# Shifting the activation pages of a transformer kernel by 32 bytes a partition

## The chip, the cores and the metric

The kernel runs on one core of one Trainium2 chip. The metric is the device time of one execution in microseconds. Before the change the median of 3 runs is 3561.03 us (3560.19 to 3562.94).

## What is computed

The reference is three transformer layers over 512 tokens of width 1024, in float32. Each of the first two layers (`hybrid_layer`) is a SwiGLU feed-forward, a mixer of three branches (a gated delta rule, a sliding-window attention, a cross attention over 256 memory rows), and a second SwiGLU, each with a layer norm. The third layer has a mixer of four attention branches and a convolutional feed-forward:

```python
def swiglu(x, w_gu, w_down):
    gate, up = jnp.split(x @ w_gu, 2, axis=-1)
    return (jax.nn.silu(gate) * up) @ w_down
...
h = layer_norm(DEEPNORM_ALPHA * x + 0.5 * swiglu(x, ffn1_w_gu, ffn1_w_down), ln_g[0], ln_b[0])
... = jnp.split(h @ w_in, split_idx, axis=-1)
merged = jnp.sum(gates * jnp.einsum('bsnc,ncd->bsnd', branches, w_branch), axis=2)
h = layer_norm(DEEPNORM_ALPHA * h + merged @ w_out, ln_g[1], ln_b[1])
return layer_norm(DEEPNORM_ALPHA * h + 0.5 * swiglu(h, ffn2_w_gu, ffn2_w_down), ln_g[2], ln_b[2])
```

Nearly all arithmetic is dense products of a weight matrix with an activation of 1024 or 2816 rows by 512 tokens.

## The kernel before

**Products.** Activations are kept transposed: a tile is 128 features (partitions) by 512 tokens, 2048 bytes a partition. A weight block is 128 by 128. Every float32 operand of a dense product is split into a rounded part (hi) and a rest (lo), both in the type float32r, and a block product is three matmuls: hi by hi, hi by lo, lo by hi. `block_matmuls` (lines 2490, 2491, 2499) issues them with 512 columns:

```python
self.e.matmul(o, hi, X.hi[kt], start=first, stop=False)
self.e.matmul(o, hi, X.lo[kt], start=False, stop=False)
...
last = self.e.matmul(o, lo, X.hi[kt], start=False, stop=final)
```

The second argument is the stationary operand (weights, from `w_hi` or `w_lo`), the third the moving operand, 128 partitions by 512 columns of a page. `pair_matmuls` (lines 2525, 2527, 2528) does the same with 256 columns, for products that are made of half tiles and sums of weight blocks; `half_matmuls` (lines 2509 to 2511) does it for the last output tile. Some blocks have two further matmuls with four columns of the tile `gains` (lines 2497, 2498). Small matmuls of attention and norms are plain float32 (lines 2473, 2478, 2536, 2568, 2596, 2609 and others).

**Memory.** `Memory.__init__` allocates the memory of each partition from low to high addresses, in the order of the code; a tensor's size is rounded up to 32 bytes. `w_lo` and `raw` (the same 14 units of 2048 bytes) begin at byte 16512, `w_hi` (9 units) at 45184, the constants `cst` at 63616. These three are multiples of 128. After `par` (1784 bytes, so 1792), `alb` (192), `small` (8192), `tab` (32), `mean_rounded` (512) and `gains` (768) come the pages: 71 tiles of 2048 bytes, each with two names, `page_f` (float32) and `page_r` (float32r). The first begins at byte 83808, which is 654 times 128 plus 96; the others follow at steps of 2048 bytes, so every page begins 96 bytes past a multiple of 128. The last ends at 229216. Nothing is allocated behind the pages.

**Who uses pages.** The moving operand of every split product is a page. ScalarE and VectorE read and write pages in norms, activations and attention. DMA touches them seldom: SyncE's queue loads the eight input tiles, the memory rows and the bias tiles and writes most of the output, ScalarE's queue moves a few half tiles. The weights go to `raw` units by 864 loads on SyncE's queue, and as pairs on SyncE's and GpSimd's.

**Order.** The work around the products is set by a planner (`Pace`) with fixed costs in the code (`BLOCK_US`, `GAIN_US`); it does not see addresses. Pages are handed out by `Stock` in the order of their numbers and of their release. A weight slab of four blocks is loaded to a `raw` unit, rounded to `w_hi` by ScalarE (line 2813), its rest written over `raw` by VectorE (line 3235), and then multiplied.

Of the kernel before, what the change touches and what calls it, by code (L numbers as in the profile page):

```python
# [13 lines left out]
P = 128  # L14
# [27 lines left out]
BESIDE = 6  # L42
HALF = (slice(0, 256), slice(256, 512))
PAGES = 71
CONST_PARTS = 4
NGAIN = 48
UNIT = SLAB * P
# [64 lines left out]
class Lane:  # L112
# [3 lines left out]
    def __init__(self, sems):  # L116
        self.tensor, self.scalar, self.vector = sems
        self.raised = [0, 0, 0]
# [311 lines left out]
class Memory:  # L430


    def __init__(self, nc, ctx, w, pairs, x_t, mem_t, consts, params, table, buckets, out):
        def sb(name, shape, dt=F32):
            return ctx.enter_context(nc.sbuf_tensor(name, shape, dt))

        def sem(name):
            return ctx.enter_context(nc.semaphore(name))

        self.pairs = pairs  # L440
        self.nc, self.w, self.x_t, self.mem_t, self.consts, self.params = nc, w, x_t, mem_t, consts, params
        self.table, self.buckets, self.out = table, buckets, out
        with nc.sbuf_tensor("w_lo", [P, NRAW * UNIT], F32R) as lo:
            self.w_lo = lo
        self.raw = sb("raw", [P, NRAW * UNIT])
        with nc.sbuf_tensor("w_lent", [P, NHI * UNIT], F32) as lent:
            self.w_lent = lent
        self.w_hi = sb("w_hi", [P, NHI * UNIT], F32R)
        self.cst = sb("cst", [P, NCONST])
        self.par = sb("par", [P, NPARAM])  # L450
        self.alb = sb("alb", [P, 48])
        self.small = sb("small", [P, 2048])
        self.tab = sb("tab", [33, 8])
        self.mean_rounded = sb("mean_rounded", [P, P], F32R)
        self.gains = sb("gains", [P, 4 * NGAIN], F32R)
        self.page_aps = []
        for i in range(PAGES):
            with nc.sbuf_tensor(f"page_r{i}", [P, 512], F32R) as r:
                rounded = r
            self.page_aps.append((sb(f"page_f{i}", [P, 512]), rounded))  # L460
        self.bank_aps = [ctx.enter_context(nc.psum_tensor(f"bank{i}", [P, 512], F32)) for i in range(8)]
        self.scratch = nc.dram_tensor("bias_rows", (8, P, 640), F32, kind="Internal").ap()

        self.lane_sems = {k: tuple(sem(f"{k}_{e}") for e in ("tensor", "scalar", "vector")) for k in LANES}
        self.s_raw = [sem(f"slab_landed{i}") for i in range(NRAW)]
        self.s_added = [sem(f"slab_added{i}") for i in range(NRAW)]
        self.s_hi, self.s_lo, self.s_gemm = sem("slab_rounded"), sem("slab_rest"), sem("blocks_multiplied")
        self.s_cst, self.s_par, self.s_tab = sem("consts_landed"), sem("params_landed"), sem("table_landed")
        self.s_x = [sem(f"x_landed{i}") for i in range(8)]
        self.s_mem = [sem(f"mem_landed{i}") for i in range(8)]  # L470
        self.s_onehot, self.s_keys, self.s_out = sem("onehot_landed"), sem("keys_landed"), sem("out_written")
        self.s_rows = [sem(f"bias_rows_written{i}") for i in range(8)]
        self.s_tile = [sem(f"bias_tile_landed{i}") for i in range(8)]
# [10 lines left out]
class Order:  # L484
# [739 lines left out]
    def prepare_memory(self):  # L1224
        for i in range(CONST_PARTS):
            self.load_constants(i)
# [1241 lines left out]
class Tensor(Engine):  # L2468
# [12 lines left out]
    def constants_ready(self):  # L2481
        self.wait_ge(self.m.s_cst, 16 * CONST_PARTS)

# [297 lines left out]
class Scalar(Engine):  # L2781
# [16 lines left out]
    def constants_ready(self):  # L2798
        self.wait_ge(self.m.s_cst, 16 * CONST_PARTS)
        self.wait_ge(self.m.s_par, 16)  # L2800
# [406 lines left out]
class Vector(Engine):  # L3207
# [6 lines left out]
    def constants_ready(self):  # L3214
        a, n = PARAM_AT["ln_b"]
        self.wait_ge(self.m.s_cst, 16 * CONST_PARTS)
        self.wait_ge(self.m.s_par, 16)
# [585 lines left out]
class Sync(Engine):  # L3803
# [11 lines left out]
    def load_constants(self, i):  # L3815
        a, b = i * NCONST // CONST_PARTS, (i + 1) * NCONST // CONST_PARTS
        self.e.dma_start(self.m.cst[:, a:b], self.m.consts[:, a:b]).then_inc(self.m.s_cst, 16)
        if i == 0:
            self.e.dma_start(self.m.par[:, :], self.m.params).then_inc(self.m.s_par, 16)
            self.wait_ge(*self.setup["table"])  # L3820
            self.e.dma_start(self.m.tab[0:32, :], self.m.table).then_inc(self.m.s_tab, 16)
# [155 lines left out]
```

## Time and profile before

| | us |
|---|---|
| median of 3 runs | 3561.03 |
| lowest, highest | 3560.19, 3562.94 |
| span of the profiled execution | 3557.1 |
| TensorE busy | 3502.0 |
| VectorE busy | 2226.9 |
| ScalarE busy | 1679.6 |

The profile is of one execution. Its page gives the span from first to last instruction and no separate time for that execution; the median lies 3.9 us above the span, which is what lies around it. The ends of matmuls are modelled, so a matmul's duration in the profile is not its share of the engine; the distance from one start to the next is.

### The profile page before, as it was taken

The numbers are of one execution on the slowest core, as the hardware profiler recorded it, in microseconds if no ns is written. First come the engines' busy times: TensorE is split into PE (matmuls) and PEld (weight loads), VectorE is DVE, ScalarE is ACT, GpSimd is POOL, SyncE is SP. The second block draws the span as 40 slices with busy tenths as digits, with TensorE's granted clock in tenths as the row PEclk, the third lists the DMA queues.
The fourth block names the chain that finished last, engine by engine and source line by source line (L and its number), as shares of the span: only waits on it lengthen the run. The fifth ranks groups of instructions, "written<-read, shape, count | busy, mean of one in ns | idle before, by whom it ended". The sixth has DMA issues, their size and how long they took to land.

```text
span 3557.1 us, 49763 instructions
## 1 busy us (share of the span) xinstructions
PE 3502.0 (98%) x19256; PEld 2932.2 (82%) x19256; DVE 2226.9 (63%) x4229; ACT 1679.6 (47%) x3243; POOL 111.3 (3%) x132
## 2 busy tenths in 40 slices
PE   9999999999999999999999999999999999999999
PEld 7898878877888987998888877888977677788887
DVE  5566656556775667566665566765676786666643
ACT  5354455554353545454555543553455443444432
POOL 0010000000000100010000000001000000000000
PEclk9999999999999999999999999999999999999999
DMA  5474331112335743574221112255522222233332
GB/s 154 131 175 143 116 95 48 45 47 72 90 105 138 173 122 98 140 172 125 83 66 47 47 60 91 93 134 151 152 79 86 69 66 84 77 94 93 95 95 86
DMA packets 198276, 358.86 MB, mean 101 GB/s; under 512 B 22102, under 2 KB 26359, under 8 KB 198040
## 3 DMA queue, kind: packets, MB, share of 16 engines
q1 hardware_dynamic: 178840, 321.32, 29.8%
q0 software_dynamic: 18432, 33.56, 5.6%
q8 instruction: 153, 2.51, 0.3%
q10 hardware_dynamic: 768, 0.79, 0.1%
q14 instruction: 83, 0.68, 0.1%
HBM read 350.60 MB, written 4.72 MB: 100 GB/s over the span
## 4 chain that ended last, share of the span: by engine, by line
PE 93%; DVE 4%; ACT 2%; issue 1%; DMA 0%; DVEq 0%; ACTq 0%
PE bank L2490 21%; PE bank L2499 21%; PE bank L2491 21%; PE bank L2525 6%; PE bank L2527 6%; PE bank L2528 6%; PE bank L2478 2%; PE bank L2473 1%; PE bank L2568 1%; PE bank L2661 1%; PE bank L2671 1%; PE bank L2536 1%; PE bank L2759 1%; PE bank L2588 1%; DVE w_lo L3235 0%
## 5 line engine op out<-in xcount | busy, mean ns | idle before, releaser
L2490 PE MATMUL bank<-page_r,w_hi 128*128 128x512 f32 (+1 forms) x3446 | 1383.4, 401 | 21.9 <-DVE w_lo L3235 14.7
L2499 PE MATMUL bank<-page_r,w_lo 128*128 128x512 f32 (+1 forms) x3446 | 1359.7, 395 | 0.0
L2491 PE MATMUL bank<-page_r,w_hi 128*128 128x512 f32 (+1 forms) x3446 | 1349.8, 392 | 0.0
L2490 PEld LDWEIGHTS bank<-page_r,w_hi 128*128 128x128 f32 x3446 | 650.0, 189 | 182.5 <-DVE w_lo L3235 18.8
L2813 ACT ACTIVATE w_hi<-raw 128x512 fp32r<-128x512 f32 x864 | 532.8, 626 | 558.3 <-PE bank L2499 550.1
L2499 PEld LDWEIGHTS bank<-page_r,w_lo 128*128 128x128 f32 x3446 | 649.2, 188 | 145.7
L2491 PEld LDWEIGHTS bank<-page_r,w_hi 128*128 128x128 f32 x3446 | 649.9, 189 | 141.6 <-issue 3.6
L3235 DVE TENSOR_TENSOR w_lo<-raw,w_hi 128x512 fp32r<-128x512 f32 x864 | 574.9, 686 | 150.2 <-ACT w_hi L2813 149.8
L2525 PE MATMUL bank<-page_r,w_hi 128*128 128x256 f32 x1792 | 503.7, 281 | 2.5 <-DVE w_lo L3253 2.5
L2528 PE MATMUL bank<-page_r,w_lo 128*128 128x256 f32 x1792 | 503.4, 281 | 0.0
L2527 PE MATMUL bank<-page_r,w_hi 128*128 128x256 f32 x1792 | 503.4, 281 | 0.0
L2525 PEld LDWEIGHTS bank<-page_r,w_hi 128*128 128x128 f32 x1792 | 337.7, 188 | 3.9 <-ACT page_f L2842 3.2
L2527 PEld LDWEIGHTS bank<-page_r,w_hi 128*128 128x128 f32 x1792 | 337.6, 188 | 0.7
L2528 PEld LDWEIGHTS bank<-page_r,w_lo 128*128 128x128 f32 x1792 | 337.7, 188 | 0.0
L3325 DVE SCALAR_TENSOR_TENSOR page_f<-bank,page_f 128x512 f32<-128x512 f32 x96 | 66.3, 691 | 261.6 <-PE bank L2499 260.6
L3253 DVE TENSOR_TENSOR w_lo<-raw,w_hi 128x1024 fp32r<-128x1024 f32 x192 | 228.8, 1220 | 0.0
L2822 ACT ACTIVATE w_hi<-raw 128x1024 fp32r<-128x1024 f32 x192 | 202.2, 1056 | 43.0 <-DVE raw L3247 21.3
L3799 POOL DMA_DIRECT2D raw<-pairs x128 | 111.1, 892 | 2425.4 <-DMA raw<-pairs 2424.0
L2842 ACT ACTIVATE page_f<-bank 128x256 f32<-128x256 f32 x128 | 49.2, 384 | 208.5 <-PE bank L2528 208.5
L2885 ACT ACTIVATE page_f<-page_f 128x512 f32<-128x512 f32 (+1 forms) x81 | 48.4, 604 | 130.8 <-DVE page_f L3325 112.6
L3776 DVE SCALAR_TENSOR_TENSOR page_f<-bank,par,page_f 128x511 f32<-128x511 f32 x88 | 65.5, 749 | 60.7 <-ACT page_f L3195 59.1
L2982 ACT ACTIVATE page_f<-bank 128x256 f32<-128x256 f32 (+3 forms) x129 | 45.4, 392 | 104.8 <-PE bank L2478 104.5
(322 smaller groups left out, 3462.9 us busy)
## 6 DMA issues: line engine op xcount, KB each, us to landing
raw<-weights SPq DMA_DIRECT2D x864, 256.0 KB, 2.7
raw<-pairs SPq DMA_DIRECT2D x320, 256.0 KB, 3.3
raw<-pairs POOLq DMA_DIRECT2D x128, 256.0 KB, 5.8
page_f<-x_t SPq DMA_DIRECT2D x8, 256.0 KB, 5.2
bias_rows<-page_f SPq DMA_DIRECT2D x8, 256.0 KB, 2.0
page_f<-bias_rows SPq DMA_DIRECT2D x8, 256.0 KB, 3.9
out_t<-page_f SPq DMA_DIRECT2D x12, 128.0 KB, 1.8
cst<-consts SPq DMA_DIRECT2D x4, 272.0 KB, 3.5
```

The lines of the kernel that those rows point to most:

```text
L2478: last = self.e.transpose(b.tile(i), ap[:, i * P:(i + 1) * P], self.const("ident"))
L2490: self.e.matmul(o, hi, X.hi[kt], start=first, stop=False)
L2491: self.e.matmul(o, hi, X.lo[kt], start=False, stop=False)
L2499: last = self.e.matmul(o, lo, X.hi[kt], start=False, stop=final)
L2525: self.e.matmul(b.cols(256), hi.r[:, c], x_hi, start=first and kt == 0, stop=False, skip_group_check=not first)
L2527: self.e.matmul(b.cols(256), hi.r[:, c], x_lo, start=False, stop=False, skip_group_check=not first)
L2528: last = self.e.matmul(b.cols(256), lo.r[:, c], x_hi, start=False, stop=kt == 3, skip_group_check=not first)
L2813: self.e.activation(hi.r, raw.f, ACT.Copy).then_inc(self.m.s_hi, 1)
L2822: self.e.activation(dst[0].wide_rounded(), src[0].wide(), ACT.Copy).then_inc(p.prep.lane.scalar, 1)
L3235: self.e.tensor_tensor(raw.r, raw.f, hi.r.bitcast(F32), ALU.subtract).then_inc(self.m.s_lo, 1)
L3253: self.e.tensor_tensor(src[0].wide_rounded(), src[0].wide(), hi[0].wide_rounded().bitcast(F32), ALU.subtract).then_inc(p.prep.lane.vector, 1)
L3799: self.e.dma_start(unit.f, self.m.pairs[p.number, QUARTERS.index(part)], accum_op=ALU.add) \
```

## The change

A tile `line_end` of 8 float32 values a partition (32 bytes) is allocated between `gains` and the pages. No instruction reads or writes it. The first page begins at byte 83840, which is 655 times 128 (327 times 256, plus 128), and each following page 2048 bytes later; the last ends at 229248. No instruction is added, removed or moved.

```diff
@@ -42,6 +42,7 @@
 PAGES = 71
+LINE_END = 8
 CONST_PARTS = 4
@@ -453,6 +454,7 @@
         self.mean_rounded = sb("mean_rounded", [P, P], F32R)
         self.gains = sb("gains", [P, 4 * NGAIN], F32R)
+        self.line_end = sb("line_end", [P, LINE_END])
         self.page_aps = []
```

## Rows read from the trace of the kernel before

**Rows 1.** The page, parts 1 and 2: busy time of the engines, granted clock in 40 slices.
```profile
PE 3502.0 (98%) x19256; PEld 2932.2 (82%) x19256; DVE 2226.9 (63%) x4229; ACT 1679.6 (47%) x3243; POOL 111.3 (3%) x132
...
PEclk9999999999999999999999999999999999999999
```

**Rows 2.** The page, part 4: chain of work that ended last, by engine and line.
```profile
PE 93%; DVE 4%; ACT 2%; issue 1%; DMA 0%; DVEq 0%; ACTq 0%
PE bank L2490 21%; PE bank L2499 21%; PE bank L2491 21%; PE bank L2525 6%; PE bank L2527 6%; PE bank L2528 6%; PE bank L2478 2%; PE bank L2473 1%; PE bank L2568 1%; PE bank L2661 1%; PE bank L2671 1%; PE bank L2536 1%; PE bank L2759 1%; PE bank L2588 1%; DVE w_lo L3235 0%
```

**Rows 3.** Groups by line and shape: the split matmuls, xcount, busy us, mean ns.
```profile
L2490 PE MATMUL bank<-page_r,w_hi 128*128 128x512 f32 x3318 | 1347.1, 406 | 20.0 <-DVE w_lo L3235 12.7 <-DVE page_f L3511 2.7 <-DVE page_r L3449 2.5
...
L2525 PE MATMUL bank<-page_r,w_hi 128*128 128x256 f32 x1792 | 503.7, 281 | 2.5 <-DVE w_lo L3253 2.5
...
L2490 PE MATMUL bank<-page_r,w_hi 128*128 128x256 f32 x128 | 36.3, 284 | 1.9 <-DVE w_lo L3235 1.9
...
L2509 PE MATMUL bank<-page_r,w_hi 128*128 128x256 f32 x20 | 5.8, 290 | 0.0
```

**Rows 4.** Timeline of TensorE, 512 columns a matmul: start us, duration, line, count.
```profile
1469.45 0.39 PE L2490 MATMUL bank<-page_r,w_hi 128*128 128x512 f32 x1
...
1481.35 0.40 PE L2490 MATMUL bank<-page_r,w_hi 128*128 128x512 f32 x1
```

**Rows 5.** Timeline of TensorE, 256 columns a matmul, same columns.
```profile
1420.15 0.28 PE L2525 MATMUL bank<-page_r,w_hi 128*128 128x256 f32 x1
...
1429.73 0.28 PE L2525 MATMUL bank<-page_r,w_hi 128*128 128x256 f32 x1
```

**Rows 6.** Busy time by engine in these two stretches, with granted clock and DMA share.
```profile
1469.45:1481.35 11.90, 11.90 (x53) 9.59 (x52) 4.21 (x7) 3.44 (x6) 0.00 (x0) 1.00 0.33 107
1420.15:1429.74 9.59, 9.59 (x84) 9.59 (x83) 7.05 (x10) 5.42 (x9) 1.76 (x2) 1.00 0.81 238
```

**Rows 7.** Chain of waits in order of time: start us, us, what.
```profile
0.74 2.78 DMA page_f<-x_t
...
510.70 1.72 PE bank L2609 x4
...
551.46 1.78 PE bank L2473 x16
554.39 0.89 PE bank L2596 x8
555.28 0.89 PE bank L2473 x8
```

**Rows 8.** Groups by line and shape: ScalarE and VectorE on weights and on pages.
```profile
L3235 DVE TENSOR_TENSOR w_lo<-raw,w_hi 128x512 fp32r<-128x512 f32 x864 | 574.9, 686 | 150.2 <-ACT w_hi L2813 149.8
L2813 ACT ACTIVATE w_hi<-raw 128x512 fp32r<-128x512 f32 x864 | 532.8, 626 | 558.3 <-PE bank L2499 550.1 <-PE bank L2528 4.1 <-DMA raw<-weights 3.1
...
L3307 DVE SCALAR_TENSOR_TENSOR page_r<-page_f,page_r 128x512 fp32r<-128x512 f32 x64 | 43.9, 687 | 5.7 <-ACT page_r L2855 5.7
...
L2855 ACT ACTIVATE page_r<-page_f 128x512 fp32r<-128x512 f32 x64 | 39.9, 624 | 28.9 <-DVE page_f L3302 28.9
...
L3776 DVE SCALAR_TENSOR_TENSOR page_f<-bank,par,page_f 128x511 f32<-128x511 f32 x44 | 32.9, 748 | 59.1 <-ACT page_f L3195 59.1
...
L3338 DVE SCALAR_TENSOR_TENSOR page_f<-page_f,par 128x512 f32<-128x512 f32 x40 | 29.6, 751 | 1.1
```

**Rows 9.** DMA issues: tile, queue, count, size, median us to landing.
```profile
raw<-weights SPq DMA_DIRECT2D x864, 256.0 KB, 2.7
...
page_f<-x_t SPq DMA_DIRECT2D x8, 256.0 KB, 5.2
```


## Prediction

> **What bounds the kernel.** I read the page's engine line first. TensorE is busy for 3502.0 of 3557.1 us, VectorE for 63% and ScalarE for 47%, and the granted clock is full in every slice, so the engine runs at its 2.4 GHz level nearly throughout [rows 1]. Busy matmuls are not matmuls at their peak, so the chain of work comes next: 93% of it lies on TensorE, and the six lines of the split products alone hold 21 + 21 + 21 + 6 + 6 + 6 = 81% [rows 2]. Nothing else can be worth much, unless it changes how long one of these matmuls holds the engine. The groups give their number: 3 x 3318 = 9954 with 512 columns, and 3 x (1792 + 128 + 20) = 5820 with 256, together 15,774 [rows 3] (each row is the first line of its group of three). Every one of them reads its moving operand from a page, so every one is touched by the change.
>
> The last view is the timeline, for the distance between starts. In a stretch without waits 51 matmuls of 512 columns take 1481.35 - 1469.45 = 11.90 us, 233.3 ns each [rows 4]; 81 matmuls of 256 columns take 1429.73 - 1420.15 = 9.58 us, 118.3 ns each [rows 5]. The clock was full in both [rows 6]. At one column a cycle of 2.4 GHz they would take 213.3 and 106.7 ns. The excess is 20.0 and 11.6 ns. It nearly doubles with the length: 8.4 ns for the 256 further columns (1024 bytes), 1.05 ns per 128 bytes, and 3.2 ns are left for a matmul of no length. A plain float32 matmul of 512 columns takes 1.72 / 4 = 430 ns [rows 7], two cycles a column (426.7) and 3.3 ns: the fixed part is there and the part that grows is not. So something in a stream of one column a cycle costs 1.05 ns per 128 bytes, and the question is whether it hangs on where the stream begins.
>
> **The change part by part.** It removes no instruction, adds none and moves none in any queue, and the planner sees no addresses. What is left is the effect of an address that goes from 96 to 0 past a multiple of 128.
>
> VectorE and ScalarE: they already work on both kinds of address. The rest of a slab, in `raw` and `w_hi` at multiples of 128, takes VectorE 686 ns, the same shape on pages 687; ScalarE's rounding takes 626 ns there and 624 on pages; a conv tap that starts 4 bytes into a page takes 748 ns, an unshifted operation with a column scalar 751 [rows 8]. I take 0. The bounds are 2 ns of some 650 either way on the 6% of the chain (213 us) that is theirs, 0.7 us.
>
> DMA: only the first input tile lies on the chain, 2.78 us [rows 7], against a median of 2.7 us for weight loads of the same size into `raw` [rows 9]. I take 0, bounds 0.1 us either way; the median of 5.2 us for all eight input tiles [rows 9] is of loads queued beside weight loads at the start, and the planner has work while they land.
>
> Plain float32 matmuls: eight of line 2596, whose moving operand is a constant at a multiple of 128, take 0.89 us, and eight of line 2473, whose moving operand is a page, take 0.89 us just behind them [rows 7]. I take 0; this pair sees a weight load of 111 ns at least as much as the stream, so it says little of split matmuls.
>
> Split matmuls: no row shows one whose moving operand begins at a multiple of 128. The bounds are nothing of the part that grows, and all of it. All of it is 16 x 1.05 = 16.8 ns for 512 columns: 9954 x 16.8 = 167 us. For 256 columns it is 8.4 ns, but the weight loads set a floor: matmuls of 128 columns follow one another at 1.78 / 16 = 111.3 ns [rows 7], which leaves 118.3 - 111.3 = 7.0 ns, and 5820 x 7.0 = 41 us. The other end is a loss, priced below at 26 us. I take 0: the nearest rows are those of the other engines and of line 2596, and none of them changes with the address; a cost that is the same for each 128 bytes of length is most simply a limit of the stream itself. The sum is 3557.1 + 0 = 3557.1 us of span, with the 3.9 us around it the median of 3561.0.
>
> The Trainium skill speaks against the change too: "SBUF — State Buffer", Specifications, gives the memory lines of 16 bytes, and 96 is a multiple of 16, so by that rule a page begins at a line before and after. By it the sum is 0 as well; whether 16 bytes are what counts, no row here shows.
>
> **Rivals.** A, the forecast: nothing changes, 3561.0.
>
> B, one line less. The cost of 1.05 ns is paid for each 128-byte line that a matmul touches. From 96 a page's 2048 bytes touch 17 lines and a half page 9; from 0 they touch 16 and 8. Each matmul saves 1.05 ns: 15,774 x 1.05 = 17 us, 3544.4. If the whole excess of 20.0 ns is 16 crossings, it is 1.25 ns and 20 us, 3541. For it: the excess follows 128 bytes of length well. Against it: it would follow a mere rate as well, and with 17 and 9 lines the fixed part would be 2.1 ns, not the 3.3 of the float32 row.
>
> C, the start costs it all. Each 32 columns are fetched as a piece that straddles two lines when a page starts off a line, and the 1.05 ns are that straddle: 167 + 41 = 208 us less, 3353. For it: the split stream asks for twice the bytes a cycle of any other, so only it would show this. ScalarE and VectorE would keep up: VectorE is busy 7.05 of 9.59 us in the densest stretch [rows 6]. Against it: no other reader shows a trace of a start's cost.
>
> The Trainium skill gives a bare matmul gap of N/2.4 + 2.5 ns ("TensorE: Matmul & The Clock Gate", Back-to-back issue gap). That is 216 ns for 512 columns and 109 for 256; an estimate from it and the counts above is 3334 us if the address is what keeps this kernel from it. The rows here stand 17 and 9 ns above that page.
>
> D, a new collision, slower. Pages, `raw`, `w_hi` and the constants would now all begin at the same place of a 128-byte line, and weight loads run beside the moving stream: they are busy 9.59 of 9.59 us with 256 columns and 9.59 of 11.90 with 512 [rows 6]. The denser stretch costs 118.3 - 233.3 / 2 = 1.7 ns more than its share. If both streams in step cost every matmul another 1.7 ns, it is 15,774 x 1.7 = 27 us, 3588. It decides from the point where the spacing of 512 columns leaves 233.3 ns upwards. Against it: the 1.7 ns may just be half of the fixed 3.2.
>
> That the pad does not do what it says (the pages stay at 96) gives A's time and is counted there.
>
> **How the numbers follow.** A 0.42, B 0.26, C 0.13, D 0.12; 0.07 is left for something between (a part of C 0.03, an unseen nothing 0.02, a smaller loss 0.02). Faster by over 0.2% (7 us, about what a measurement of this kernel can tell from no change) is 0.26 + 0.13 + 0.03 = 0.42, within it 0.44, slower 0.14. The time is that of A. A alone would give 3556 to 3566. The range takes in B with its dearer price (3541) and D (3588), from 3540 to 3589, and leaves out C and what lies near it.
>
> **What would show it.** The distance between starts in the stretches of [rows 4, 5]: 233.3 and 118.3 ns by A, some 232.2 and 117.2 by B, 216.5 and 111.3 by C, 235 and 120 by D, all at full clock. TensorE's busy time would move with the median and the idle time before it would not. VectorE's 687 and ScalarE's 624 ns on pages should stand. The forecast is wrong if the spacing of the 512-column matmuls moves by over 0.5 ns, and the reasoning is wrong if the time moves while the spacing stands.

## The result, and the profile after

The changed kernel takes 3520.28 us (median of 4 runs, 3520.00 to 3524.52) against 3560.61 for the kernel before beside it: ratio 0.989, 95% interval 0.9877 to 0.9903, 40 us less. The forecast was no change, with a range of 3540 to 3589; both are wrong. Rivals B (3544) and C (3353) had the sign, D named the two streams that turn out to matter but gave them the other sign, and no rival had the cause. One execution of e2_page64 below took 6929.6 us, far from all others of any kernel, and is left out of its median.

The page of the changed kernel, whose code lines stand two further down than before. Part 1 (busy us, share, count), and part 4 (the chain), for [rows 1, 2]; the groups of part 5 stand below by shape:

```profile
PE 3457.2 (98%) x19256; PEld 2940.1 (84%) x19256; DVE 2226.0 (63%) x4229; ACT 1681.5 (48%) x3243; POOL 111.5 (3%) x132
...
PE 91%; DVE 5%; ACT 3%; issue 1%; DMA 0%; DVEq 0%; SPq 0%; ACTq 0%
```

TensorE has the same 19,256 matmuls and is busy 44.8 us less; VectorE and ScalarE have their times of before. The profiled execution took 3520.0 us, 1.8 more than its span of 3518.2; so of the 3.9 us between median and span before the change, about 2 are the difference between one execution and the next, and not time around the span.

Groups by line and shape of the changed kernel (count, busy us, mean ns, idle before), for [rows 3, 8]:

```profile
L2492 PE MATMUL bank<-page_r,w_hi 128*128 128x512 f32 x3318 | 1331.5, 401 | 23.4 <-DVE w_lo L3237 15.9 <-DVE page_f L3513 2.7 <-DVE page_r L3451 2.5
L2527 PE MATMUL bank<-page_r,w_hi 128*128 128x256 f32 x1792 | 507.3, 283 | 2.4 <-DVE w_lo L3255 2.4
L3309 DVE SCALAR_TENSOR_TENSOR page_r<-page_f,page_r 128x512 fp32r<-128x512 f32 x64 | 43.8, 685 | 5.7 <-ACT page_r L2857 5.7
L2857 ACT ACTIVATE page_r<-page_f 128x512 fp32r<-128x512 f32 x64 | 39.9, 624 | 28.5 <-DVE page_f L3304 28.5
L3778 DVE SCALAR_TENSOR_TENSOR page_f<-bank,par,page_f 128x511 f32<-128x511 f32 x44 | 32.9, 748 | 53.5 <-ACT page_f L3197 53.5
```

The mean of the 512-column matmuls falls from 406 to 401 ns and that of the 256-column ones rises from 281 to 283. The two shapes moved in opposite directions, which no rival had. VectorE and ScalarE on pages stand at 685, 624 and 748 ns.

The timeline of TensorE in two stretches without waits, first and last start of 51 matmuls with 512 columns and of 81 with 256, for [rows 4, 5]:

```profile
3215.05 0.39 PE L2492 MATMUL bank<-page_r,w_hi 128*128 128x512 f32 x1
...
3226.61 0.39 PE L2492 MATMUL bank<-page_r,w_hi 128*128 128x512 f32 x1
```

```profile
200.13 0.28 PE L2527 MATMUL bank<-page_r,w_hi 128*128 128x256 f32 x1
...
209.85 0.28 PE L2527 MATMUL bank<-page_r,w_hi 128*128 128x256 f32 x1
```

That is 11.56 / 51 = 226.7 ns instead of 233.3, and 9.72 / 81 = 120.0 instead of 118.3. In cycles of 2.4 GHz: 544 instead of 560, 288 instead of 284. With the counts of the prediction it is 9954 x 6.67 = 66 us saved and 5820 x 1.67 = 10 us lost, 57 in all if every matmul stood in such a stretch.

Where the other 17 us are: the sum of all distances between starts, by shape, tells it. Distances of at most 240 ns behind a 512-column matmul sum to 2149.5 us against 2206.1 (56.6 less: between other work they do not settle at 226.7, and the mean of neighbours is 227.6). Longer distances, which hold the waits, sum to 194.8 against 185.5 (9.3 more). All behind 256-column matmuls sum to 709.8 against 700.7 (9.1 more), the rest to 451.7 against 452.3. Together that is 38.8 us less, and the span fell by 38.9. One place of the 9.3 us is the wait for the weights' rest, which comes sooner behind a shorter stream; the waits of TensorE for it (us in total, times, longest), first of the kernel before, then after:

```profile
PE bank L2490 <- DVE w_lo L3235: 14.7, 11, 5.6
```

```profile
PE bank L2492 <- DVE w_lo L3237: 17.9, 11, 5.5
```

### The profile page after: what moved, and what is told of

Its sections match the earlier page's. It is cut to its first block, busy times and chain, and to the rows that moved or that the text cites. A ratio compares the mean times of both kernels' runs of the same rounds, so it can differ in the third digit from the quotient of the medians.

```text
span 3518.2 us, 49763 instructions
## 1 busy us (share of the span) xinstructions
PE 3457.2 (98%) x19256; PEld 2940.1 (84%) x19256; DVE 2226.0 (63%) x4229; ACT 1681.5 (48%) x3243; POOL 111.5 (3%) x132
## 4 chain that ended last, share of the span: by engine, by line
PE 91%; DVE 5%; ACT 3%; issue 1%; DMA 0%; DVEq 0%; SPq 0%; ACTq 0%
PE bank L2492 21%; PE bank L2501 21%; PE bank L2493 20%; PE bank L2527 6%; PE bank L2530 6%; PE bank L2529 6%; PE bank L2480 2%; PE bank L2475 1%; PE bank L2570 1%; PE bank L2663 1%; DVE w_lo L3237 1%; PE bank L2673 1%; PE bank L2538 1%; DVE page_r L3279 1%; PE bank L2590 1%
## 5 line engine op out<-in xcount | busy, mean ns | idle before, releaser
L2492 PE MATMUL bank<-page_r,w_hi 128*128 128x512 f32 (+1 forms) x3446 | 1367.9, 397 | 25.4 <-DVE w_lo L3237 17.9
L2501 PE MATMUL bank<-page_r,w_lo 128*128 128x512 f32 (+1 forms) x3446 | 1343.4, 390 | 0.0
L2493 PE MATMUL bank<-page_r,w_hi 128*128 128x512 f32 (+1 forms) x3446 | 1332.1, 387 | 0.0
L3801 POOL DMA_DIRECT2D raw<-pairs x128 | 111.3, 894 | 2406.0 <-DMA raw<-pairs 2404.2
```

Source lines behind the costliest of these rows:

```text
L3801: self.e.dma_start(unit.f, self.m.pairs[p.number, QUARTERS.index(part)], accum_op=ALU.add) \
```

## The experiments

**Pads of other sizes.** The only edit is the size of `line_end`:

```diff
-LINE_END = 8
+LINE_END = 16    # e1_page32; 24 in e2_page64, 32 in e3_page96_moved
```

For e4_page0_of_256, whose pages begin at a multiple of 256 instead of 128 past one, the tile `alb` moves behind the pages and the pad is 24 values:

```diff
-        self.alb = sb("alb", [P, 48])
...
             self.page_aps.append((sb(f"page_f{i}", [P, 512]), rounded))
+        self.alb = sb("alb", [P, 48])
```

e1_page32. 

> A pad of 64 bytes instead of 32: pages begin 32 bytes past a multiple of 128. Line theory (a matmul pays for 128-byte lines, and only a start at a multiple of 128 is free of the extra cost): spacing of the 512-column matmuls 233.3 ns and of the 256-column ones 118.3 ns as with 96, time 3561 us. 64-byte theory (only the start within 64 bytes counts, and 32 is as bad as 96): the same, 3561 us. Partial theory (the cost falls with the number of columns in the first, cut line: 24 here against 8 with 96): something between 226.7 and 233.3 ns, time between 3520 and 3561 us.

Measured: 3552.23 us, ratio 0.998 (0.9971 to 0.999). The 512-column matmuls stay at 233.3 ns, the 256-column ones stand at 117.8 and 116.7 instead of 118.3.

e2_page64. 

> A pad of 96 bytes: pages begin 64 bytes past a multiple of 128. Line theory: 233.3 and 118.3 ns, 3561 us. 64-byte theory: as with 0, 226.7 and 120.0 ns, 3520 us. Partial theory: between.

Measured: 3524.95 us (median of 3), ratio 0.9895 (0.9879 to 0.9912).

e3_page96_moved. 

> A pad of 128 bytes: pages lie 128 bytes higher than before the change, again 96 past a multiple of 128. Line theory and 64-byte theory: 233.3 and 118.3 ns, 3561 us. Rival (any shift of the pages against the weights or the end of memory brings the gain, whatever the remainder): 226.7 ns, 3520 us.

Measured: 3571.59 us, ratio 1.0034 (1.0022 to 1.0045). The kernel has the very remainder of before and is slower than before, so a shift by itself does not bring the gain either.

e4_page0_of_256. 

> Pages begin at a multiple of 256 bytes (byte 83712), where the changed kernel has 128 past one; the 192 bytes of the tile alb lie behind the pages instead of ahead. Line theory: as the changed kernel, 226.7 and 120.0 ns, 3520 us. Rival (longer lines of 256 bytes, of which the change got half): spacing of 512 columns below 225 ns, time below 3510 us.

Measured: 3557.23 us, ratio 0.9993 (0.9984 to 1.0003). Pages begin at a multiple of 256, thus of 128, and the gain is gone.

The timelines of e4_page0_of_256 and of e2_page64, again 51 matmuls apart:

```profile
3215.68 0.39 PE L2492 MATMUL bank<-page_r,w_hi 128*128 128x512 f32 x1
...
3227.58 0.40 PE L2492 MATMUL bank<-page_r,w_hi 128*128 128x512 f32 x1
```

```profile
3215.58 0.39 PE L2492 MATMUL bank<-page_r,w_hi 128*128 128x512 f32 x1
...
3227.25 0.39 PE L2492 MATMUL bank<-page_r,w_hi 128*128 128x512 f32 x1
```

233.3 ns in the first, although its pages are aligned; 228.9 in the second, although they are not. The remainder by 128 does not order the six kernels, so the line theory, the 64-byte theory and the longer line all fall. The partial theory falls as well: it makes a start at 32 (24 columns in the cut line) better than one at 64 (16 columns), and e1 is 27 us slower than e2. What was left was an address counted from something else. The weights begin at byte 16512 and 45184, both 128 past a multiple of 256.

**The same address, another distance.** Against the kernel before, weights and pages both move up by 32 bytes in the first kernel; in the second weights move by 96 and pages by 128. The edit against the changed kernel:

```diff
+AHEAD_OF_WEIGHTS = 8     # e5; 24 in e6
...
+        self.ahead = sb("ahead", [P, AHEAD_OF_WEIGHTS])
         with nc.sbuf_tensor("w_lo", [P, NRAW * UNIT], F32R) as lo:
...
-        self.line_end = sb("line_end", [P, LINE_END])     # taken out in e5 only
```

e5_weights32_page0. 

> The pad of 32 bytes stands ahead of the weights instead of ahead of the pages: weights, constants and pages all move up 32 bytes. Pages begin at the very address of the changed kernel (83840, a multiple of 128), and the distance from the weights to the pages is that of the kernel before. Address theory (the remainder of the page's address decides): spacing 226.7 and 120.0 ns, 3520 us. Distance theory (the moving stream and the weight load get into each other's way by the distance of their addresses, modulo 256 or 512): 233.3 and 118.3 ns, 3560 us.

Measured: 3560.66 us, ratio 0.9999 (0.999 to 1.0009).

e6_weights96_page96. 

> 96 bytes ahead of the weights and 32 ahead of the pages: pages begin 96 past a multiple of 128 (byte 83936, the address at which the pad of 128 bytes gave 233.3 and 120.0 ns and 3571 us), the distance from the weights is that of the changed kernel. Address theory: 233.3 and 120.0 ns, 3571 us. Distance theory: 226.7 and 120.0 ns, 3520 us.

Measured: 3522.78 us, ratio 0.9896 (0.9881 to 0.9911). First and last start of 51 matmuls, e5 and then e6:

```profile
3215.55 0.40 PE L2493 MATMUL bank<-page_r,w_hi 128*128 128x512 f32 x1
...
3227.44 0.40 PE L2493 MATMUL bank<-page_r,w_hi 128*128 128x512 f32 x1
```

```profile
3215.38 0.39 PE L2494 MATMUL bank<-page_r,w_hi 128*128 128x512 f32 x1
...
3226.94 0.39 PE L2494 MATMUL bank<-page_r,w_hi 128*128 128x512 f32 x1
```

233.3 and 226.7 ns. The pages of e5 begin at exactly the byte of the changed kernel, at a multiple of 128, and it has the time of the kernel before. The pages of e6 begin 96 bytes past one and it has the changed kernel's time. The alignment of the pages is worth nothing; their distance from the weights is what decides.

**TensorE alone.** A small kernel of its own, which ran once, repeats the two streams with every other engine idle. `wo` and `po` are the offsets w and p in float32 values, `EACH` is 48. Its core:

```python
for n, wo, po in groups():
    e.matmul(banks[3][:, 0:4], wts[:, 256:384], mov[:, 0:4], start=True, stop=True)
    for i in range(EACH):
        o = banks[bank][:, 0:n]
        last = e.matmul(o, wts[:, wo:wo + 128], mov[:, po:po + n], start=i % 24 == 0, stop=i % 24 == 23)
...
```

m1_streams. 

> A kernel of its own, which computes nothing of the reference: after 144 matmuls to warm up, groups of 48 float32r matmuls one behind the other with a weight load each, the other engines idle. Weights begin at a multiple of 512 bytes plus w, the moving operand at one plus p. Distance theory: the spacing follows p - w; with 512 columns p = 0 gives 226.7 ns and p = 96 or 224 gives 233.3; w = p = 32 and w = p = 96 are as w = p = 0; with 256 columns 120.0 ns at 0 and 118.3 at 224. Address theory: it follows p alone. Rival that it is the other engines' traffic: every group at 512 columns takes the same, near 216 ns.

Its timeline (48 matmuls a row, 512 columns; the four-column matmul of line 65 parts the groups). The five groups have w = 0 and p = 0, 32, 64, 96 and 128 bytes:

```profile
47.26 11.18 PE L68 MATMUL bank<-mov,wts 128*128 128x512 f32 x48
58.27 0.17 PE L65 MATMUL bank<-mov,wts 128*128 128x4 f32 x1
58.30 11.44 PE L68 MATMUL bank<-mov,wts 128*128 128x512 f32 x48
69.58 0.17 PE L65 MATMUL bank<-mov,wts 128*128 128x4 f32 x1
69.61 11.24 PE L68 MATMUL bank<-mov,wts 128*128 128x512 f32 x48
80.69 0.17 PE L65 MATMUL bank<-mov,wts 128*128 128x4 f32 x1
80.72 11.44 PE L68 MATMUL bank<-mov,wts 128*128 128x512 f32 x48
92.00 0.17 PE L65 MATMUL bank<-mov,wts 128*128 128x4 f32 x1
92.03 11.40 PE L68 MATMUL bank<-mov,wts 128*128 128x512 f32 x48
```

and those with w = p = 32, w = p = 96, and w = 32 with p = 0:

```profile
319.07 11.18 PE L68 MATMUL bank<-mov,wts 128*128 128x512 f32 x48
...
330.12 11.15 PE L68 MATMUL bank<-mov,wts 128*128 128x512 f32 x48
...
341.13 11.45 PE L68 MATMUL bank<-mov,wts 128*128 128x512 f32 x48
```

Equal offsets give 11.15 to 11.18 us wherever they are; moving the weights alone by 32 bytes gives 11.45. The spacing in the settled part of each group (from its seventh matmul on), beside the kernels:

| distance (page less weights, modulo 256 bytes) | kernel, us | its 512 / 256 columns, ns | TensorE alone, ns |
|---|---|---|---|
| 0 | after 3520.3, e6 3522.8 | 226.7 / 120.0 | 227.0 / 120.0 |
| 32 | e1 3552.2 | 233.3 / 117.8 (116.7 in later stretches) | 233.3 / 116.8 |
| 64 | e2 3525.0 | 228.9 / 117.8 (113.3 in one stretch) | 228.9 / 113.3 |
| 96 | e3 3571.6 | 233.3 / 120.0 | 233.4 / 120.1 |
| 128 | e4 3557.2 | 233.3 / 118.7 | 232.2 / 118.6 |
| 160 | | | 234.2 / 117.3 |
| 192 | | | 233.4 / 113.3 |
| 224 | before 3560.6, e5 3560.7 | 233.3 / 118.3 | 233.4 / 118.3 |

Distances of 256 to 480 bytes repeat those of 0 to 224 to 0.3 ns, so the pattern has a period of 256 bytes. Distances of 4, 8 and 16 bytes take 236.7, 233.4 and 231.4 ns. The spacing neither rises nor falls steadily with the distance, and it is another one for each length: 0 is the best distance for 512 columns and among the worst for 256. With 384 columns distances 0, 224 and 256 all take 173.3 to 173.5 ns, and with 128 columns, 53.3 ns of stream, all take 111.7: there something else than the stream sets the pace, most likely the weight load. That the other engines play no part is shown by their being idle here.

The table also gives the times: e3 differs from the kernel before only in the 256-column matmuls, 5820 x 1.67 = 10 us more by spacing, and was 12.5 us above the kernel before beside it.

**Triples and narrower weights.** The second small kernel, which also ran once, takes hi and lo tiles at four distances each, as the split products do, and then 64 and 32 columns of weights:

```diff
+                    e.matmul(o, hi, mov[:, p1:p1 + n], start=i % 24 == 0, stop=False)
+                    e.matmul(o, hi, mov[:, 1024 + p2:1024 + p2 + n], start=False, stop=False)
+                    last = e.matmul(o, lo, mov[:, p1:p1 + n], start=False, stop=i % 24 == 21)
```

m2_triples. 

> A kernel of its own, which computes nothing of the reference, in groups of 48 matmuls like the split products: hi weights by a hi tile at p1, hi weights by a lo tile at p2, lo weights at b by the hi tile at p1, each offset one of 0, 64, 128 and 192 bytes from a multiple of 256; and the same with 64 and 32 columns of weights instead of 128. Distance theory with the weight load as the other stream: each matmul's excess over its columns follows the distance of its moving tile from the weights that are loaded beside it, 32 cycles of 2.4 GHz at most and at least as in the single groups (512 columns: 32 at distance 0; 256 columns: 16 at 64 and 192), so 256 columns with all at 64 take 113.3 ns; with half the weight columns the excess halves (512 columns at distance 0: about 220 ns instead of 226.7), with a quarter it is 8 to 12 cycles, and the difference between distances 0 and 224 shrinks with it from 6.7 ns to under 2. Rival, the moving stream alone pays for crossing lines: 226.7 and 233.3 ns whatever the width of the weights.

Measured, as the mean of the last 33 distances of a group: for 512 columns the best of 64 triples is the one with everything at distance 0, 226.7 ns; the others lie at 227.8 to 235.5, up to 53 cycles over their columns where 32 at most was expected. For 256 columns three of 64 take 113.3 ns, three more 115.5, and most lie between 117 and 120; the triple with all at 64, expected at 113.3, took 117.8 here. That narrow weights halve the excess failed. The timeline of the group with 32 columns of weights at distance 0, 33 matmuls apart:

```profile
1232.78 0.39 PE L74 MATMUL bank<-mov,wts 128*32 128x512 f32 x1
...
1240.42 0.40 PE L74 MATMUL bank<-mov,wts 128*32 128x512 f32 x1
```

It is 7.64 / 33 = 231.5 ns, where less than 220 was expected. At 64 columns of weights it is 229.8. With 256 columns it goes the other way: the same kind of group with 64 columns of weights at distance 0, 33 matmuls apart:

```profile
1265.11 0.28 PE L76 MATMUL bank<-mov,rest 128*64 128x256 f32 x1
...
1268.85 0.28 PE L76 MATMUL bank<-mov,rest 128*64 128x256 f32 x1
```

That is 3.74 / 33 = 113.3 ns, as with 32 columns, against 120.0 with 128. So at distance 0 a narrower weight load costs more beside 512 columns and less beside 256, and the theory that counts collisions by the columns loaded is wrong. What did shrink, as expected, is the difference between distances 0 and 224 for 512 columns: 2.0 ns with 64 columns of weights (231.8 against 229.8) and, with the sign turned round, 1.7 with 32 (229.9 against 231.6). The rival, that the moving stream pays alone, is wrong as well, as it has 226.7 whatever the width. The width changes the pattern, so the weight load is in it; how a collision is counted stays open.

Two groups of the same 256-column triple, all at distance 64, differ only in two or three matmuls sent ahead of them. First and last start, 33 matmuls apart:

```profile
1143.34 0.28 PE L74 MATMUL bank<-mov,wts 128*128 128x256 f32 x1
...
1147.08 0.28 PE L74 MATMUL bank<-mov,wts 128*128 128x256 f32 x1
...
1149.39 0.28 PE L74 MATMUL bank<-mov,wts 128*128 128x256 f32 x1
...
1153.28 0.28 PE L74 MATMUL bank<-mov,wts 128*128 128x256 f32 x1
```

113.3 and 117.9 ns: the two streams settle in one of two patterns by how they begin. Of ten such groups, five at distance 64 and five at 192, six took 113.3 and four 117.8. The same is seen in e2_page64, where three of the four long stretches of pairs stay at 117.8 ns, and the one that begins at 1518 us leaves it at one late matmul:

```profile
1538.17 0.28 PE L2530 MATMUL bank<-page_r,w_lo 128*128 128x256 f32 x1
1538.29 0.35 PE L2527 MATMUL bank<-page_r,w_hi 128*128 128x256 f32 x1
1538.47 0.28 PE L2529 MATMUL bank<-page_r,w_hi 128*128 128x256 f32 x1
...
1540.06 0.28 PE L2527 MATMUL bank<-page_r,w_hi 128*128 128x256 f32 x1
```

From 1538.47 to 1540.06 there are 14 distances of 113.6 ns, and it stays there for over 700 matmuls.

**A version that beats both?** The best distance for 512 columns is 0 and for 256 it is 64 or 192. The last 16 pages get 64 more bytes ahead of them, and the sums of half tiles, which only 256-column matmuls read, take these pages first:

```diff
+            if i == PAGES - APART:
+                self.step = sb("step", [P, 16])     # left out in e8
...
-        return self.slots.pop(0)
+        i = next((i for i, x in enumerate(self.slots) if x.apart == apart), 0)
+        return self.slots.pop(i)
...
-            a, b, ha, hb = (self.pages.take() for _ in range(4))
+            a, b, ha, hb = (self.pages.take(True) for _ in range(4))
```

e7_sums_apart. 

> The changed kernel with 64 more bytes ahead of its last 16 pages, which the sums of half tiles take first (Stock.take has a preference); 2726 of the 5376 matmuls of the pairs then read a page at distance 64 from the weights, the rest and nearly all of 512 columns stay at distance 0. Distance theory: the 2726 take 117.8 or 113.3 ns by the phase they fall into, instead of 120.0, so the time is 6 to 18 us below the changed kernel's 3520 us: 3502 to 3514. Rival (a stream settles only over many matmuls of one distance, and switching every 12 keeps it unsettled): no gain, 3520 us or more.

Measured: 3520.20 us, ratio 0.9891 (0.9874 to 0.9907), where the distance theory had 3502 to 3514.

e8_sums_together. 

> The same preference in handing out pages, without the 64 bytes: all pages at distance 0. It tells what the other order of pages costs by itself. Both theories: 120.0 and 226.7 ns, 3520 us within 5.

Measured: 3523.07 us, ratio 0.99 (0.9885 to 0.9914). The 64 bytes bring 2.9 us against e8: the ratios' intervals overlap, but the slowest of the four executions of e7 (3520.52) is faster than the fastest of e8 (3521.38). Against the changed kernel they bring nothing that can be told.

The rival, that switching every 12 matmuls keeps the stream unsettled, does not fit the trace. The trace does not name the page of a matmul, but in e7 stretches of twelve (four triples) stand out by their spacing. One of them, and the return to 120.0 ns:

```profile
202.70 0.28 PE L2536 MATMUL bank<-page_r,w_lo 128*128 128x256 f32 x1
...
203.88 0.29 PE L2533 MATMUL bank<-page_r,w_hi 128*128 128x256 f32 x1
204.01 0.28 PE L2535 MATMUL bank<-page_r,w_hi 128*128 128x256 f32 x1
204.12 0.29 PE L2536 MATMUL bank<-page_r,w_lo 128*128 128x256 f32 x1
204.25 0.28 PE L2533 MATMUL bank<-page_r,w_hi 128*128 128x256 f32 x1
204.36 0.28 PE L2535 MATMUL bank<-page_r,w_hi 128*128 128x256 f32 x1
```

The first of the twelve, at 202.46, takes 122 ns. From 202.70 to 203.88 there are 10 distances of 117.8. The four distances from 203.88 to 204.36 are 128, 117, 125 and 114, together 484 against 4 x 120, and then it is 120 again. So these short runs do settle, within a matmul or two, at the 117.8 ns of distance 64; no six distances in a row of the pairs come near the other pattern, 113.3. All distances behind 256-column matmuls sum to 705.6 us against 709.7 in e8, 4.1 less, where 2726 x 2.2 = 6 us was the least expected; each switch takes back some 4 ns going in and 4 coming out. Longer distances behind 512-column matmuls, which hold the waits, take back another 3.5 us (198.3 against 194.8). The distance theory had the spacing right in its poorer case and overrated what it is worth.

## Why the prediction was wrong

Right were the parts that were costed at nothing and are nothing: VectorE, ScalarE, DMA and plain float32 matmuls. The chain in order of time of the changed kernel, for [rows 7] (start us, us, what):

```profile
0.74 2.67 DMA page_f<-x_t
...
506.20 1.72 PE bank L2611 x4
...
554.13 1.78 PE bank L2475 x16
```

The plain float32 matmuls take 1.72 and 1.78 us as before, and the first tile lands after 2.67 us instead of 2.78. Right too was where the effect would have to lie, in the distance between starts of the 15,774 split matmuls, with the time following it.

Wrong was the step "Split matmuls", at "I take 0". The nearest rows were those of other engines and of line 2596, and none of those readers runs two streams at a column a cycle beside a weight load; they could not tell. By spacing it is worth 57 us. The bounds, from a gain of 208 us to a loss of 26 (rival D's own product, 15,774 x 1.7, is 27), held it, and the text gave the rows of another kind of reader more weight than they bear.

Also wrong was the reading behind it, "a cost that is the same for each 128 bytes of length is most simply a limit of the stream itself". It rested on two lengths, 20.0 and 11.6 ns. After the change the excess is 13.3 ns for either length, 32 cycles, and does not grow at all; and with TensorE alone 384 columns at distance 224, that of the kernel before, take 173.4 ns, where the reading gives 160 + 3.2 + 12 x 1.05 = 175.8. The growing part of 1.05 ns per 128 bytes and the fixed 3.2 ns were a line through two points that happen to belong to two settled patterns.

Rival B had the sign and predicted 232.2 and 117.2 ns; it was 226.7 and 120.0. Rival C priced 216.5 and 111.3 ns for a start at a line; e4 and e5 start at one and gain nothing, e6 starts off one and gains all. Rival D, "a new collision", named the two streams that do meet and priced it at 1.7 ns, which is what the 256-column matmuls lost; it took the sign of one shape for both, and the agreement in size is luck, as its reason for 1.7 ns (the share of the denser stretch) was another. The change's own account, that pages at a multiple of 128 bytes are read better, falls with e4 and e5.

## What to carry to other kernels

When matmuls with a weight load each stand back to back and their spacing is above columns over clock, shift the moving tiles against the weights by 32 bytes at a time through 256 and read the spacing for each length of matmul; a pad takes no instruction, and its sign cannot be told from alignment. Only float32r operands were tried here. Any change that shifts an allocation by other than a multiple of 256 bytes can move such a kernel by over 1% (the six distances tried here span 3520 to 3572 us), so a change of another kind that also moves memory is to be compared at the same distance. Choose the distance by the shape that holds most of the time. A second distance for short runs of another shape works only in part: in e7 it held its spacing, but switching and waits took most of it back.

## What the runs showed of the hardware

I had not expected that the pace of matmuls with a weight load each depends on the distance between the addresses of moving operand and weights, modulo 256 bytes: 226.7 to 236.7 ns for 512 columns and 113.3 to 120.1 for 256 in the single groups, with every other engine idle. The Trainium skill says of TensorE's two read ports that they are independent and that "PE and ACT never wait on anyone" ("SBUF — State Buffer", Who interferes with whom); these runs do not agree as far as TensorE's own two readers go, though they do not tell whether the ports or the memory behind them is where they meet. The gap of N/2.4 + 2.5 ns that the Trainium skill gives ("TensorE: Matmul & The Clock Gate", Back-to-back issue gap), 216 ns for 512 columns, was reached at no distance: the best was 226.7, at full clock.

Nor had I expected that the same code at the same addresses has two steady paces, 113.3 and 117.8 ns, by how the stream begins.
